# Three edits to a two-block transformer kernel: banks that signal one by one, low halves shared with VectorE, and weight strips multiplied in two passes

## The reference

```python
def peer(h, w_query, sub_keys1, sub_keys2, expert_u, expert_v):
    ...
    v1, i1 = lax.top_k(s1, PEER_TOPK)
    v2, i2 = lax.top_k(s2, PEER_TOPK)
    cand = (v1[..., :, None] + v2[..., None, :]).reshape(T, PEER_HEADS, PEER_TOPK * PEER_TOPK)
    vc, ic = lax.top_k(cand, PEER_TOPK)
    e1 = jnp.take_along_axis(i1, ic // PEER_TOPK, axis=-1)
    e2 = jnp.take_along_axis(i2, ic % PEER_TOPK, axis=-1)
    idx = (e1 * N_KEYS + e2).reshape(T, PEER_HEADS * PEER_TOPK)
    gate = jax.nn.softmax(vc, axis=-1).reshape(T, PEER_HEADS * PEER_TOPK)
    def block(args):
        xb, ib, gb = args
        u = expert_u[ib]
        pre = jnp.einsum('td,tkd->tk', xb, u).astype(jnp.float32)
        a = jax.nn.gelu(pre, approximate=False) * gb
        return jnp.einsum('tk,tkd->td', a, expert_v[ib])
...
for layer in range(DEPTH):
    ...
    x = x + mixed
    hn = rmsnorm(x, ffn_norm[layer])
    x = x + (jax.nn.silu(hn @ ffn_w_gate[layer]) * (hn @ ffn_w_up[layer])) @ ffn_w_down[layer]
```

## Time and profile before

| what | value |
|---|---|
| runs of the kernel | 1641.84, 1643.02, 1645.74 us; median 1643.02 |
| profiled execution, own time | 1644.6 us |
| its span (first to last instruction) | 1642.7 us |
| granted TensorE clock, mean | 0.984 |
| TensorE busy | 1570.3 us (96%), 11771 matmuls |
| VectorE, ScalarE, GpSimd busy | 1119.9, 833.6, 297.4 us |
| strips | 489, 512 KB each |
| HBM read | 262.75 MB, 161 GB/s over the span |

### The profile page before, as it was taken

One profiled execution on the slowest core, in us unless ns is written; L12 is line 12 of the kernel. 1 busy time (PEld: TensorE's weight loads), 2 busy tenths in 40 slices (PEclk: granted clock), 3 DMA queues, 4 the chain that ended last, 5 costly groups with the idle time before them and its releaser, 6 DMA issues.

```text
span 1642.7 us, 33077 instructions
## 1 busy us (share of the span) xinstructions
PE 1570.3 (96%) x11771; PEld 1428.6 (87%) x11771; DVE 1119.9 (68%) x2154; ACT 833.6 (51%) x1241; POOL 297.4 (18%) x122
## 2 busy tenths in 40 slices
PE   6868999999999999999999989999999999999999
PEld 6757999998889999888899989999998777778887
DVE  7686666634666666576599970288877999975555
ACT  6456434457854344756456556544444444445553
POOL 2001000064210000100368898500000000000000
PEclk9879999999999999999999999999999999999999
DMA  6104556553365565333545545554554545555554
GB/s 219 65 32 143 183 181 191 183 164 102 123 202 184 184 191 181 123 121 103 172 162 170 170 148 188 171 166 165 166 166 146 174 166 169 171 166 194 194 192 154
DMA packets 72558, 264.70 MB, mean 161 GB/s; under 512 B 8080, under 2 KB 8336, under 8 KB 72112
## 3 DMA queue, kind: packets, MB, share of 16 engines
q1 hardware_dynamic: 71744, 261.00, 48.8%
q10 hardware_dynamic: 752, 2.83, 0.5%
HBM read 262.75 MB, written 1.05 MB: 161 GB/s over the span
## 4 chain that ended last, share of the span: by engine, by line
PE 83%; POOL 5%; DVE 5%; issue 3%; ACT 3%; DMA 0%; POOLq 0%; DVEq 0%; SPq 0%; ACTq 0%
PE ps L508 26%; PE ps L510 24%; PE ps L509 24%; POOL w_lo L2326 5%; PE ps L1026 2%; DVE arena L1547 1%; PE ps L687 1%; DVE w_lo L1547 1%; ACT xn L1140 0%; PE ps L615 0%; DVE x_s L1547 0%; PE ps L851 0%; ACT arena L1246 0%; DVE hT_lo L1585 0%; ACT hT_hi L1128 0%
## 5 line engine op out<-in xcount | busy, mean ns | idle before, releaser
L1101 ACT ACTIVATE w_hi<-ring 128x1024 fp32r<-128x1024 f32 x489 | 515.4, 1057 | 344.8 <-PE ps L510 329.3
L508 PE MATMUL ps<-hT_hi,w_hi 128*128 128x256 f32 x2216 | 638.5, 288 | 22.1 <-POOL w_lo L2326 9.7
L509 PE MATMUL ps<-hT_hi,w_lo 128*128 128x256 f32 x2216 | 627.5, 283 | 0.0
L510 PE MATMUL ps<-hT_lo,w_hi 128*128 128x256 f32 x2216 | 627.2, 283 | 0.0
L1547 DVE TENSOR_TENSOR w_lo<-ring,w_hi 128x1024 fp32r<-128x1024 f32 x376 | 458.6, 1220 | 91.2 <-ACT w_hi L1101 88.7
L508 PEld LDWEIGHTS ps<-hT_hi,w_hi 128*128 128x128 f32 x2216 | 425.2, 192 | 29.6 <-issue 10.5
L509 PEld LDWEIGHTS ps<-hT_hi,w_lo 128*128 128x128 f32 x2216 | 425.6, 192 | 1.6
L2326 POOL TENSOR_TENSOR w_lo<-ring,w_hi 128x1024 fp32r<-128x1024 f32 x113 | 288.8, 2573 | 754.9 <-ACT w_hi L1101 745.6
L510 PEld LDWEIGHTS ps<-hT_lo,w_hi 128*128 128x128 f32 x2216 | 425.2, 192 | 0.0
L508 PE MATMUL ps<-w_hi,halves_hi 128*128 128x512 f32 x688 | 275.6, 401 | 3.4 <-DVE halves_lo L1547 3.4
L510 PE MATMUL ps<-w_lo,halves_hi 128*128 128x512 f32 x688 | 269.4, 392 | 0.0
(11 more groups left out here) (267 smaller groups left out, 1326.3 us busy)
## 6 DMA issues: line engine op xcount, KB each, us to landing
ring<-in_strips SPq DMA_DIRECT2D x489, 512.0 KB, 3.5
const<-in_const SPq DMA_DIRECT2D x1, 1352.0 KB, 11.5
x_s<-in_x SPq DMA_DIRECT2D x2, 512.0 KB, 4.4
arena<-in_rel ACTq DMA_DIRECT2D x1, 1024.0 KB, 4.8
arena<-in_keys ACTq DMA_DIRECT2D x1, 1024.0 KB, 6.2
out<-x_s SPq DMA_DIRECT2D x4, 256.0 KB, 2.1
arena<-in_ssm_bc SPq DMA_DIRECT2D x1, 512.0 KB, 6.6
arena<-in_ssm_b SPq DMA_DIRECT2D x1, 512.0 KB, 7.9
```

The source lines that it names most:

```text
L508: pe.matmul(out, l_hi, r_hi, start=start, stop=False, **kw)
L509: pe.matmul(out, l_lo, r_hi, start=False, stop=False, **kw)
L510: return pe.matmul(out, l_hi, r_lo, start=False, stop=stop, **kw)
L1101: sc.activation(w_hi[:, n % RING, :], ring[:, n % RING, :], ACT.Copy).then_inc(high_ready, 1)
```

## The change

1. The last strip of each stage signals each of its first three banks (`part_done`), and `residual` waits for one bank at a time.
2. In the key lookup, VectorE does one low half after each of its 12 lookup instructions: strips 260, 262, ... 282. GpSimd does 261, 263, ... 283, and each of the two waits until the strip before its own is out.
3. TensorE waits for the high half only (`high_ready`), does all products with it, then waits for the low half (`low_halves`) and does the rest. The last strips of the stages (`last`) keep their order and wait for both halves first; `glu` waits for both too.

```diff
@@ -37,6 +37,7 @@
 NE1 = 128
 HALF = NE1 // 2
 OWN_LOWS = HALF + 2
+SHARED_LOWS = (27, 51)
 GATE_UP = 2.0 ** 15
 EPS = 1e-6
 BIG = 1e30
@@ -306,7 +307,7 @@
         strip_landed = [sem(f"strip_landed{i}") for i in range(RING)]
-        first_half = sem("first_half")
+        part_done = sem("part_done")
         strip_done = sem("strip_done")
         high_ready = sem("high_ready")
         low_ready = sem("low_ready")
@@ -500,8 +501,13 @@
         def _(pe):
             def split(n, i=None):
+                pe.wait_ge(high_ready, n + 1 if i is None else UNROLL * i + (n + 1))
+                return w_hi[:, n % RING, :], w_lo[:, n % RING, :], n, i
+
+            def low_halves(w):
+
+                n, i = w[2:]
                 pe.wait_ge(low_ready, n + 1 if i is None else UNROLL * i + (n + 1))
-                return w_hi[:, n % RING, :], w_lo[:, n % RING, :]
             def mm3(out, l_hi, l_lo, r_hi, r_lo, start, stop, **kw):
@@ -519,8 +525,12 @@
                 for c in range(KC):
                     input_ready(fresh, c)
                     cols = slice(c * P, (c + 1) * P)
-                    mm = mm3(out, w[0][:, cols], w[1][:, cols], hT_hi[:, c, :], hT_lo[:, c, :],
-                             c == 0, c == KC - 1)
+                    pe.matmul(out, w[0][:, cols], hT_hi[:, c, :], start=c == 0, stop=False)
+                    pe.matmul(out, w[0][:, cols], hT_lo[:, c, :], start=False, stop=False)
+                low_halves(w)
+                for c in range(KC):
+                    mm = pe.matmul(out, w[1][:, c * P:(c + 1) * P], hT_hi[:, c, :], start=False,
+                                   stop=c == KC - 1)
                 mm.then_inc(strip_done, 1)
             nproj = [0]
@@ -548,10 +558,17 @@
                         for c in range(4):
                             input_ready(fresh, 4 * half + c)
                             cols, tok = slice(c * T, (c + 1) * T), slice(a * P, (a + 1) * P)
-                            mm = mm3(ps[:, b, a * T:(a + 1) * T], hT_hi[:, 4 * half + c, tok],
-                                     hT_lo[:, 4 * half + c, tok], w[0][:, cols], w[1][:, cols],
-                                     half == 0 and a == 0 and c == 0, half == 1 and c == 3,
-                                     skip_group_check=True)
+                            o = ps[:, b, a * T:(a + 1) * T]
+                            pe.matmul(o, hT_hi[:, 4 * half + c, tok], w[0][:, cols],
+                                      start=half == 0 and a == 0 and c == 0, stop=False, skip_group_check=True)
+                            pe.matmul(o, hT_lo[:, 4 * half + c, tok], w[0][:, cols], start=False, stop=False,
+                                      skip_group_check=True)
+                    low_halves(w)
+                    for a in range(NT):
+                        for c in range(4):
+                            cols, tok = slice(c * T, (c + 1) * T), slice(a * P, (a + 1) * P)
+                            mm = pe.matmul(ps[:, b, a * T:(a + 1) * T], hT_hi[:, 4 * half + c, tok], w[1][:, cols],
+                                           start=False, stop=half == 1 and c == 3, skip_group_check=True)
                     mm.then_inc(strip_done, 1)
             def raw_norm(i):
@@ -591,14 +608,25 @@
             def rows(w, hi, lo, first, last):
+                if last:
+                    low_halves(w)
                 for a in range(NT):
                     for b in range(2):
                         tok, cols = slice(a * P, (a + 1) * P), slice(b * 512, (b + 1) * 512)
-                        mm = mm3(ps[:, 2 * a + b, :], hi[:, tok], lo[:, tok], w[0][:, cols],
-                                 w[1][:, cols], first, last, skip_group_check=True)
-                    if last and a == 0:
-
-                        mm.then_inc(first_half, 1)
+                        o = ps[:, 2 * a + b, :]
+                        pe.matmul(o, hi[:, tok], w[0][:, cols], start=first, stop=False)
+                        pe.matmul(o, lo[:, tok], w[0][:, cols], start=False, stop=False)
+                        if last:
+                            mm = pe.matmul(o, hi[:, tok], w[1][:, cols], start=False, stop=True)
+                        if last and not (a and b):
+
+                            mm.then_inc(part_done, 1)
+                if not last:
+                    low_halves(w)
+                    for a in range(NT):
+                        for b in range(2):
+                            tok, cols = slice(a * P, (a + 1) * P), slice(b * 512, (b + 1) * 512)
+                            mm = pe.matmul(ps[:, 2 * a + b, :], hi[:, tok], w[1][:, cols], start=False, stop=False)
                 mm.then_inc(strip_done, 1)
             def out_rows(i, name, ns, order=range(KC), slots=range(KC)):
@@ -740,6 +768,7 @@
                 def glu(cs):
                     w = [split(AT[("even", "glu", n)]) for n in range(2)]
+                    low_halves(w[1])
                     for c in cs:
                         pe.wait_ge(y_low, c + 1)
                         for n in range(2):
@@ -1563,11 +1592,11 @@
             def residual(i):
                 for a in range(NT):
-                    if a == 0:
-                        ve.wait_ge(first_half, i)
-                    else:
-                        ve.wait_ge(strip_done, AT[LASTS[i - 1]] + 1)
                     for b in range(2):
+                        if a and b:
+                            ve.wait_ge(strip_done, AT[LASTS[i - 1]] + 1)
+                        else:
+                            ve.wait_ge(part_done, 3 * (i - 1) + 2 * a + b + 1)
                         v = x_s[:, a, b * 512:(b + 1) * 512]
                         tt(v, v, ps[:, 2 * a + b, :], ALU.add).then_inc(x_ready, 1)
@@ -2200,6 +2229,16 @@
                 ch.link(ve.tensor_copy(r_if.rearrange("p a s b -> p (a s b)"),
                                        iu.rearrange("p a s b -> p (a s b)")))
                 ch.link(ve.tensor_copy(r_hlf.rearrange("p a b -> p (a b)"), hl.rearrange("p a b -> p (a b)")))
+                shared = iter(range(AT[("peer", "u", 0)] + SHARED_LOWS[0], AT[("peer", "u", 0)] + SHARED_LOWS[1], 2))
+
+                def beside(ins):
+
+                    ch.add(ins)
+                    n = next(shared)
+                    ve.wait_ge(low_ready, n)
+                    low(n)
+                    ch.wait()
+
                 big = [P, PH, TOPK, TOPK]
                 tmp = keys_s.rearrange("p a b -> p (a b)").rearrange(
                     "p (h k i) -> p h k i", h=PH, k=TOPK)
@@ -2208,9 +2247,9 @@
                     for part in range(2):
                         at = r_hlf[:, part, a * P:(a + 1) * P].rearrange("p (h k) -> p h k", h=PH)
                         keys = r_if[:, a, part:2 * PH:2, :]
-                        ch.link(tt(tmp, at.unsqueeze(3).broadcast_to(big), iota16, ALU.is_equal))
-                        ch.link(tt(tmp, tmp, keys.unsqueeze(2).broadcast_to(big), ALU.mult))
-                        ch.link(ve.tensor_reduce(
+                        beside(tt(tmp, at.unsqueeze(3).broadcast_to(big), iota16, ALU.is_equal))
+                        beside(tt(tmp, tmp, keys.unsqueeze(2).broadcast_to(big), ALU.mult))
+                        beside(ve.tensor_reduce(
                             r_e[:, part, a * P:(a + 1) * P].rearrange("p (h k) -> p h k", h=PH), tmp, AX,
                             ALU.add))
                 ve.wait_ge(route_act, 1)
@@ -2354,7 +2393,18 @@
             for n in range(2 * PH):
                 low(base + n)
             base = AT[("peer", "u", 0)]
-            with po.Fori(0, OWN_LOWS // UNROLL) as i:
+            first, last = SHARED_LOWS
+            with po.Fori(0, first // UNROLL) as i:
+                for e in range(UNROLL):
+                    low(base + e, i)
+            for e in range(first // UNROLL * UNROLL, first):
+                low(base + e)
+            for e in range(first + 1, last, 2):
+                po.wait_ge(low_ready, base + e)
+                low(base + e)
+            for e in range(last, -(-last // UNROLL) * UNROLL):
+                low(base + e)
+            with po.Fori(-(-last // UNROLL), OWN_LOWS // UNROLL) as i:
                 for e in range(UNROLL):
                     low(base + e, i)
```

## The result

The changed kernel takes **1628.84 us** (median of 4 runs, 1627.24 to 1632.66), against 1644.38 us of the kernel before in the same session: ratio **0.9915**, 95% interval 0.9899 to 0.9930 (the two medians alone divide to 0.9905, inside it). The forecast was 1626.2, with a range of 1621 to 1635. The profiled execution has a span of 1625.4 us and 1627.24 of its own, 17.4 less than the 1644.6 of before, where 16.8 was forecast. The total is nearly right, in part by luck: in this pair of profiles some 4 us of the 17.4 are a stretch at half clock that the changed kernel does not have, and the edits give about 13.6.

The account below looks back on a forecast made before the run. TensorE, 96% busy, was taken to bound the kernel, so only closing its holes pays. 10.2 + 3.9 + 3.8 + 2.0 - 3.1 = 16.8 us off 1644.6 gives 1627.8, less 1.6 to the median: 1626.2 us, range 1621 to 1635.

Parts of the forecast that it names:

- Part 1: Key lookup: sharing low halves between VectorE and GpSimd closes TensorE's holes from 930 to 976 us; gain 10.2 us.
- the first tight hole: Lookup's start: GpSimd's strip 259 ends near 935.6, wanted at 933.9; two passes cover it to 935.8. Hole 1.57 + 0.16 us.
- The cover for VectorE's delay: Lookup ends near 1005 us instead of 973, but TensorE takes its result only near 1055; cost nothing, without cover some 32.
- Part 2: Stage ends: a signal per bank starts the additions and the square 0.65 us earlier at six places; gain 3.9 us.
- everything behind it is that chain: Stage ends: what follows ScalarE's square depends on the additions, so each 0.65 us saved there carries through.
- Part 3a: Holes at low halves in both MLPs, the mixer's head and one first-layer output strip close; gain 3.8 us.
- Part 3b: First stage: with two passes the two projection strips that wait for VectorE end sooner; gain 2.0 us, bounds 0 and 3.4.
- VectorE's chain does not hear of TensorE here: First stage: VectorE's work does not depend on TensorE's strips, its low half being done at 40.05; no size given.
- the first stage's is swallowed by its holes: First stage's head: its extra 0.72 us from two passes costs nothing, as holes there absorb it.
- Part 3c: Stage heads: 12 matmuls instead of 6 behind the input's last part, 0.72 us at four heads, 0.24 at stick-breaking; -3.1 us.
- Part 3d: Every strip's one more wait costs 0; upper bound 0.08 us, from the first matmul behind a scatter and its waits.
- three signs of being wrong: Pitches above 0.12 us at the low pass, MLP clock below 1.00, TensorE waiting for VectorE's low half in the lookup.

Follow-up runs that it names:

- turns_by_column: Heads_by_arrival, with TensorE turning the input by column blocks instead of by token tile in three stages; 0.9858 to the kernel before.
- order_only: The changed kernel, but TensorE waits for both halves before it begins a strip, keeping the two-pass order; 0.9966 to the kernel before.
- banks_again: The kernel before with only the one-signal-per-bank edit at stage ends, run a second time; 0.9973 to the kernel before.
- lookup_only: The kernel before with only the key-lookup edit, VectorE taking twelve low halves between its lookup operations; 0.9954 to the kernel before.
- Squares_last: turns_by_column, with ScalarE evacuating the normed input before both squares instead of between them; 0.9865 to the kernel before.
- heads_old: The changed kernel, but fresh strips at four heads wait for the low half first and keep the old product order; 0.9875 to the kernel before.
- mid_waits: The kernel before with two more, already satisfied, low-half waits in the middle of nearly every strip; 1.0002 to the kernel before.
- passes_only: The kernel before with only the two-pass strips, waiting for the low half between passes; 0.9964 to the kernel before.
- Heads_by_arrival: The changed kernel, but fresh strips of four stages take products in the order their input arrives; 0.9865 to the kernel before.

## Why the prediction came out

**Part 1, 10.2 us: right in the sum, and only with part 3.** All holes of the stretch for low halves are gone, which gives 10.7 us by the starts of the matmuls, and the new wait for ScalarE at 962.73 takes 0.6 back. The working already said that the two passes cover the first tight hole. It had missed that there would be a second. Alone the lookup edit gives 6.6, the two together 10. The cover for VectorE's delay held too: `route_ready` follows 987.67 within some 7 us, and TensorE takes its result up at 1043.

**Part 2, 3.9 us: too large.** The additions do start 0.68 us earlier at all six places. The step "everything behind it is that chain" failed at three of them. There TensorE's transposes are next, behind the last strip, and only 0.23 is left (turns_by_column shows it: without ScalarE's wait for them the first part comes another 0.37 us sooner, and 0.23 + 0.37 is the 0.6 of the other places). It measured 2.6 by the trace.

**Part 3a, 3.8 us: right for the MLPs, but 3.0 in all,** as 1.26 - 0.72 for the head + 0.23 of part 2 is the 0.76 that each is shorter, and 1.24 comes back when order_only brings the hole back. In the mixer the 1.02 was given back by a new wait of 0.93 + 0.16 for ScalarE. That was missed: ScalarE's list behind the fresh strip was not costed.

**Part 3b, 2.0 us: too large, and hidden by the clock.** The first stage is 5.4 us shorter in the profile. The block of 256 small matmuls that the earlier trace rows show at 52.68 now starts at 51.70, 1.0 sooner. Then the block itself takes 7.1 us from its first matmul to its last instead of 11.1, and that is the clock. Here are before, after and banks_again, which has no second pass:

```profile
52.50:64.00 11.50, 11.32 (x256) 11.34 (x256) 4.74 (x19) 2.03 (x3) 0.00 (x0) 0.63 0.15 48
51.50:59.00 7.50, 7.30 (x256) 7.26 (x256) 6.63 (x24) 2.05 (x3) 0.00 (x0) 1.00 0.12 48
52.50:60.00 7.50, 7.25 (x256) 7.26 (x256) 4.80 (x19) 2.10 (x3) 0.00 (x0) 1.00 0.18 56
```

Banks_again starts the block at 52.75 and takes 7.1 us too, so the 4.0 us are not the second pass's own work. The other 0.4 of the stage is the hole of the output strip that 3a counts. Of the six kernels that wait for the low half first, three (before, lookup_only, order_only) have the block at half clock; of the eight that start early, none. Whether the early start helps there is open.

The 1.0 is below 2.0 because the step "VectorE's chain does not hear of TensorE here" failed, with "the first stage's is swallowed by its holes". Before, VectorE makes its fourth low half of the stage at 20.40 without a wait. After and order_only:

```profile
21.58 1.23 DVE L1576 TENSOR_TENSOR w_lo<-ring,w_hi 128x1024 fp32r<-128x1024 f32 x1 [1.13 <-ACT w_hi L1130]
21.13 1.23 DVE L1576 TENSOR_TENSOR w_lo<-ring,w_hi 128x1024 fp32r<-128x1024 f32 x1 [0.62 <-ACT w_hi L1130]
```

ScalarE's high half waits for TensorE's first strip, whose two passes end 0.7 us later at full clock (order_only), and 1.2 later in after, where the clock is 0.50 from 15.4 to 18.8. VectorE's list then runs 0.5 and 0.9 us late: the low half that was taken to be out at 40.05 is out at 40.98. 1.9 - 0.9 = 1.0. Squares_last, at full clock up to the block and with its head taken by arrival, starts it at 51.24, 1.4 sooner than before.

**Part 3c, -3.1 us: right** at the five heads that it counts, 0.72 at four and 0.22 at the stick-breaking one, and the worst of the change: heads_old has four of them back at no cost. The first stage's, put at nothing, is the 0.5 us of 3b.

**Part 3d, 0: right** (mid_waits). The bound of 0.08 us came from matmuls that had nothing queued before them.

**The sum.** In place of 10.2 + 3.9 + 3.8 + 2.0 - 3.1 = 16.8 the edits show about 10.1 + 2.6 + 3.0 + 1.0 - 3.1 = 13.6, and the block at full clock adds 4.0: 17.6, against 17.4 in the profiled span. Each term that missed was too high (part 2 by 1.3, 3a by 0.8 for the mixer, 3b by 1.0), and the clock made up for them. That the profiled execution came out near the forecast is luck to that extent. The timed ratio, 14.0 us, is nearer to the edits alone; how much clock is in it no run shows.

**What the profile would show.** Of the signs of being right, the 377 matmuls (384 or so were written down), VectorE's low halves between the steps, the earlier additions and the 12 matmuls behind the last part are there; the square's start came 0.6 us nearer (138.69 in the row above, against 144.72 in the earlier trace rows), but the first normed part only 0.23 at three places; the end of the lookup was 990 and not 1005. None of the three signs of being wrong appeared.

## What to carry to other kernels

Splitting each product so that it starts on the operand that is ready first pays where an operand is late by about as much as the first pass lasts or less (where it is late at every strip, as in passes_only, it pays once), and costs where the other operand arrives in pieces: take those strips in order of arrival. Heads_by_arrival (0.9865) beats the kernel before and the changed one, though by its time it is not told apart from heads_old, and turns_by_column saves 0.36 us more at three boundaries by the trace. When a chain is shortened, look for what stands ready right behind each of its steps on every engine; here a row of transposes and table loads took back part of the gain. And a step that is made longer at a stage's head can come out of another engine's list 20 us later. Where two engines hold each other up, giving each every second item, each behind the other's signal, can remove the waits of the third, if the turns begin where both arrive. Whether giving all to the faster engine would do as well was not tried. Before a gain in one profile is put down to an edit, compare the granted clock of the same block in both.

## What was not expected of the hardware

- Stretches at half clock move between two profiles of the very same kernel (on two chips): the mixer took 138.11 and 141.19 us, with 1.00 and 0.95 granted between 650 and 720. No edit had touched it. A single profile of this kernel is therefore good to some 3 us in the first stage, the mixer and the odd stage, while the MLPs mostly repeat to 0.02.
- In the first stage TensorE waits for engines up to 10.4 us at a time, in every kernel, and the clock granted between 55 and 110 us is 0.69 to 0.78 in all of them. One block of 256 small matmuls there took 7.1 us in eleven profiles and 11.1 to 11.3 in three.
- In a row of queued matmuls a wait that is already satisfied costs TensorE less than can be measured, 0.002 us at most (mid_waits).
